# Norms between stages in halves of 512 tokens, with the first three chunks of the next stage fed half by half

## The chip, the cores and the metric

The kernel runs on one core of one Trainium2 chip. The metric is the device time of one execution in microseconds (us), the median of several; lower is better. Engines are named as in the profile: PE is TensorE (matrix products), DVE is VectorE, ACT is ScalarE, POOL is GpSimd, SP is SyncE, which issues most of the DMAs.

## The reference, cut to what matters

The program computes a chain of residual layers over 1024 tokens of width 1024, in float32. Between the large parts it only adds and norms:

```python
for layer in range(2):
    h = rmsnorm(x, mix_pre_g[layer])
    m = even_mixer(h, ...) if layer % 2 == 0 else odd_mixer(h, ...)   # forgetting attention + pooling / gated linear recurrence
    x = x + rmsnorm(m, mix_post_g[layer])
    h = rmsnorm(x, ffn_pre_g[layer])
    x = x + rmsnorm(swiglu(h, w_gate, w_up, w_down), ffn_post_g[layer])
# second block
xn = rmsnorm(x, norm_pre_g);  proj = xn @ w_in
...                                     # mLSTM branch, S5 branch, gates
x = x + rmsnorm(merged @ w_o, norm_post_g)

def rmsnorm(x, g):                      # over the 1024 channels of a token
    return x * rsqrt(mean(x * x, axis=-1) + 1e-6) * g
```

## The kernel before, in words

Activations lie transposed: channels on the 128 partitions, in KT = 8 tiles, the S = 1024 tokens along the free dimension. A product is made from three matrix products of rounded parts (`product`, lines 343 to 345): every operand is split in a high part and a low rest, `H_hi`, `H_lo` for the normed input and `w_hi`, `w_lo` for the weights. Weights come as a stream of chunks of 128x1024: SP loads a chunk into `raw[slot]` (L309), POOL splits it (L331 and L333) as soon as the chunk that used the slot before has been multiplied (semaphore `multiplied`), and PE multiplies it (`columns`): 8 tiles by 2 halves of 512 tokens by 3 products, 48 matmuls into two PSUM banks. There are three slots.

Each engine has its program as a list of stages, run in order: `prelude` (constants for later stages), then boundary b0, `fox` (attention), b1, `ffn(0)`, b2, `lru`, b3, `ffn(1)`, b4, `s5`, `mlstm`, `merge`, b5. Nothing else orders the work: each engine goes through its list, and semaphores tie the lists together.

A boundary takes the last stage's output Y, norms it (`post`), adds it to the residual X (read back from memory; X lies where H_hi and H_lo will be, in b1 in the scratch area), writes X out, norms X (`pre`) and leaves H. b0 has no `post`, b5 no `pre`. In order, for whole tiles 128x1024:

- ACT squares the tiles of Y (L410) as they come, POOL adds the first seven (L476), PE sums over the partitions by 8x8 small matmuls with `pick` (L441); ACT takes the root (L401), DVE the reciprocal (L502), PE spreads it over the partitions into PSUM (L448).
- DVE scales Y tile by tile (L515); DVE adds the even tiles to X (L518), POOL the odd ones (L487).
- ACT squares each new X (L421) and issues its store (L423); PE sums; root, reciprocal, spread again.
- POOL splits the next stage's first three chunks after its last X add.
- DVE scales X (L535), ACT rounds it to H_hi (L430), DVE (even, L529) and POOL (odd, L495) make H_lo. Four tiles of scratch go round.

The first chunk of the next stage waits on PE for each tile of H as it is finished (`ready`); the others follow whole. The next stage's ACT, DVE and, in `s5`, SP programs begin with a wait for `tmp_free`: all of H_lo made and all of X stored. In `s5` that is ahead of the loads of its maps (`s_bn`, `s_cn`) and of all its DVE work (from L1808 on); in `ffn` and `lru` ahead of a memset of Y.

`prelude` runs on DVE before b0: 77 small steps, each waiting for the one before it, then two sines on ACT (L1165, L1166), then 15 more small steps. b0's `tmp_free` condition makes its ACT, DVE and POOL programs wait for the last of them. The first chunk of `fox` holds the gate logits: ACT and DVE turn them into `negc_rows` (L799 to L801, L890 to L894), SP writes those to memory, reads them back, and only then loads chunk 4 and on. The first attention pass on DVE is L946.

Of the kernel before, what the change touches and what calls it, by code (L numbers as in the profile page):

```python
# [194 lines left out]
def block_program(nc, A, out_x):  # L195
# [169 lines left out]
    def boundary(tag, post, pre, src, y_ready, x_free, sq_free, next_chunks=None, x_at=None):  # L365


# [5 lines left out]
            (f"{tag}_spreads", [KT, KT, P], F32), (f"{tag}_roots", [KT, P], F32), (f"{tag}_inverses", [KT, P], F32), keep=14 * S * 4)  # L373
        y_sum = t1
        sq, tmp = (sq0, sq1), (t0, t1, t2, t3)
        stats = int(bool(post)) + int(bool(pre))

        totals = dict(x_loaded=16, x_even=n_post // 2, x_odd=n_post // 2, x_stored=16 * n_post, y_squared=n_post, y_summed=max(0, n_post - 1), squared=n_pre, summed=KT - 1 if pre else 0,
                      all_summed=2 * stats, rooted=stats, inverted=stats, spreads_made=1, y_scaled=n_post,
                      h_full=n_pre, h_hi=n_pre, h_even=n_pre // 2, h_odd=n_pre // 2)  # L380
# [4 lines left out]
        x_new = ("x_even", "x_odd")  # L385

        sums = [ps[0:KT, 4 + 2 * n, 0:P] for n in range(2)]
        first = 0 if post else 1

        def sp(e):  # L390
            for w, v in x_free:
                e.wait_ge(w, v)
            e.dma_start(X[:, :, :], src.rearrange("k p n -> p k n")).then_inc(q["x_loaded"], 16)

        def act(e):
            for w, v in sq_free:
                e.wait_ge(w, v)

            def root(stat):
                e.wait_ge(q["all_summed"], b["all_summed"] + 2 * (stat - first) + 1)  # L400
                e.activation(roots[:, :], sums[stat], ACT.Sqrt, scale=1.0 / D, bias=eps_col[0:KT, :]).then_inc(q["rooted"], 1)  # L401

            e.activation(warm[:, :], eps_col[:, :], ACT.Sqrt)
            if post:
                with e.Fori(0, KT // 2) as i:
                    for t in range(2):
                        k = 2 * i + t
                        e.wait_ge(y_ready[0], y_ready[1] + k + 1)
                        e.wait_ge(q["y_summed"], b["y_summed"] + k + 1)
                        e.activation(sq[t][:, :], tile(Y, k), ACT.Square).then_inc(q["y_squared"], 1)  # L410
                root(0)
            if pre:
                if not post:
                    e.wait_ge(q["x_loaded"], b["x_loaded"] + 16)
                with e.Fori(0, KT // 2) as i:
                    for t in range(2):
                        k = 2 * i + t
                        if post:
                            e.wait_ge(q[x_new[t]], b[x_new[t]] + i + 1 + 2 * t)
                        e.wait_ge(q["summed"], b["summed"] + k + 1)  # L420
                        e.activation(sq[t][:, :], tile(X, k), ACT.Square).then_inc(q["squared"], 1)  # L421
                        if post:
                            e.dma_start(tile(x_dram_t, k), tile(X, k)).then_inc(q["x_stored"], 16)  # L423
                root(1)
                if post:
                    e.wait_ge(q["x_stored"], b["x_stored"] + 16 * KT)
                with e.Fori(0, KT // 4) as i:
                    for t in range(4):
                        e.wait_ge(q["h_full"], b["h_full"] + 4 * i + t + 1)
                        e.activation(tile(H_hi, 4 * i + t), tmp[t][:, :], ACT.Copy).then_inc(q["h_hi"], 1)  # L430
            else:
                with e.Fori(0, KT // 2) as i:
                    for t in range(2):
                        e.wait_ge(q[x_new[t]], b[x_new[t]] + i + 1 + 2 * t)
                        e.dma_start(tile(out_x.rearrange("k p n -> p k n"), 2 * i + t), tile(X, 2 * i + t)).then_inc(q["x_stored"], 16)
                e.wait_ge(q["x_stored"], b["x_stored"] + 16 * KT)

        def pe(e):
            def add(stat, squares, start, stop):
                for m in range(KT):  # L440
                    ins = e.matmul(sums[stat], pick[:, m * KT:(m + 1) * KT], squares[:, m * P:(m + 1) * P], start=start and m == 0, stop=stop and m == KT - 1)  # L441
                return ins

            def spread(stat):
                e.wait_ge(q["spreads_made"], b["spreads_made"] + 1)
                e.wait_ge(q["inverted"], b["inverted"] + stat - first + 1)
                for m in range(KT):
                    ins = e.matmul(ps[:, 2 * stat + m // 4, (m % 4) * P:(m % 4 + 1) * P], spreads[:, m, :], inverses[:, :], start=True, stop=True)  # L448
                ins.then_inc(q["all_summed"], 1)

            if post:
                e.wait_ge(q["y_summed"], b["y_summed"] + KT - 1 + 2)
                e.wait_ge(y_ready[0], y_ready[1] + KT)
                add(0, y_sum, True, False)
                e.wait_ge(q["y_squared"], b["y_squared"] + KT)
                add(0, sq[1], False, True).then_inc(q["all_summed"], 1)
                spread(0)
            if pre:
                for k in range(KT):
                    e.wait_ge(q["squared"], b["squared"] + k + 1)  # L460
                    add(1, sq[k % 2], k == 0, k == KT - 1).then_inc(q["all_summed" if k == KT - 1 else "summed"], 1)
                spread(1)

        def pool(e):
            o = steps_of(e, "pool")
            for w, v in sq_free:
                e.wait_ge(w, v)

            e.tensor_tensor(spreads[:, :, :], ident[0:KT, 0:KT].rearrange("p (m o) -> p m o", o=1).broadcast_to([KT, KT, P]),
                            ones[0:KT, :].rearrange("p (o n) -> p o n", o=1).broadcast_to([KT, KT, P]), ALU.mult).then_inc(q["spreads_made"], 1)  # L470
            if post:
                o(e.memset(y_sum[:, :], 0.0))

                def sum_up(k, squares):
                    e.wait_ge(q["y_squared"], b["y_squared"] + k + 1)
                    e.tensor_tensor(y_sum[:, :], y_sum[:, :], squares[:, :], ALU.add).then_inc(q["y_summed"], 1)  # L476
                    e.wait_ge(q["y_summed"], b["y_summed"] + k + 3)

                with e.Fori(0, KT // 2 - 1) as i:
                    for t in range(2):  # L480
                        sum_up(2 * i + t, sq[t])
                sum_up(KT - 2, sq[0])
                with e.Fori(0, KT // 4) as i:
                    for t in (1, 3):
                        k = 4 * i + t
                        e.wait_ge(q["y_scaled"], b["y_scaled"] + k + 1)
                        e.tensor_tensor(tile(X, k), tile(X, k), tmp[t][:, :], ALU.add).then_inc(q["x_odd"], 1)  # L487
            if next_chunks:
                split_chunks(e, next_chunks, 0, SLOTS)
            if pre:  # L490
                with e.Fori(0, KT // 4) as i:
                    for t in (1, 3):
                        k = 4 * i + t
                        e.wait_ge(q["h_hi"], b["h_hi"] + k + 1)
# [2033 lines left out]
```

## Time and profile before

| | us |
|---|---|
| median of 3 runs | 3793.95 (3792.83 to 3794.66) |
| the profiled execution, its own time | 3794.27 |
| its span, first to last instruction | 3791.4 |
| PE busy | 3459.4 (91%) |
| PE weight loads busy | 2800.8 (74%) |
| DVE busy | 1776.6 (47%) |
| ACT busy | 731.2 (19%) |
| POOL busy | 1540.6 (41%) |
| mean granted clock of TensorE, of its full 2.4 GHz | 0.957 |

The time of an execution is some 3 us longer than the span of its instructions. Busy shares are means over stages of different kinds; matmuls overlap, so a busy PE need not be at its peak. In timelines a row gives start, duration (of all merged pieces, from the first start to the last end or their sum), engine, line, operation, tiles out and in, shape, count, and in brackets the idle time before it and what ended it.

### The profile page before, as it was taken

The numbers are of one execution on the slowest core, as the hardware profiler recorded it, in microseconds if no ns is written. First come the engines' busy times: TensorE is split into PE (matmuls) and PEld (weight loads), VectorE is DVE, ScalarE is ACT, GpSimd is POOL, SyncE is SP. The second block draws the span as 40 slices with busy tenths as digits, with TensorE's granted clock in tenths as the row PEclk, the third lists the DMA queues.
The fourth block names the chain that finished last, engine by engine and source line by source line (L and its number), as shares of the span: only waits on it lengthen the run. The fifth ranks groups of instructions, "written<-read, shape, count | busy, mean of one in ns | idle before, by whom it ended". The sixth has DMA issues, their size and how long they took to land. (4 is left out here: it accounts for less than half of the span.)

```text
span 3791.4 us, 40722 instructions
## 1 busy us (share of the span) xinstructions
PE 3459.4 (91%) x15904; PEld 2800.8 (74%) x15904; DVE 1776.6 (47%) x1746; ACT 731.2 (19%) x923; POOL 1540.6 (41%) x720
## 2 busy tenths in 40 slices
PE   6999898999999979986999999989787999989897
PEld 4777686888888867765888888868666777767685
DVE  4444425332332367675323323259665566565542
ACT  3333312000000033333100000021111223122110
POOL 4111645433443463445434433466642422413255
PEclk9999899999999999997999999989889999999998
DMA  3110022111111221121111111123212210101122
GB/s 102 40 29 26 17 84 73 51 50 50 50 44 50 89 73 39 44 89 56 51 50 50 44 50 44 50 106 89 65 52 78 87 35 28 53 22 53 33 78 105
DMA packets 246568, 215.78 MB, mean 57 GB/s; under 512 B 7988, under 2 KB 213428, under 8 KB 246472
## 3 DMA queue, kind: packets, MB, share of 16 engines
q1 hardware_dynamic: 225888, 165.14, 14.7%
q10 hardware_dynamic: 20584, 49.31, 3.7%
q8 instruction: 66, 1.08, 0.1%
q14 instruction: 30, 0.25, 0.0%
HBM read 180.78 MB, written 29.43 MB: 55 GB/s over the span
## 5 line engine op out<-in xcount | busy, mean ns | idle before, releaser
L331 POOL TENSOR_TENSOR w_hi<-raw,one_col 128x1024 fp32r<-128x1024 f32 x265 | 528.2, 1993 | 1921.2 <-PE ps L345 1866.2
L343 PE MATMUL ps<-H_hi,w_hi 128*128 128x512 f32 x2848 | 1138.7, 400 | 89.1 <-DVE H_lo L529 23.6
L345 PE MATMUL ps<-H_hi,w_lo 128*128 128x512 f32 x2848 | 1119.4, 393 | 0.0
L344 PE MATMUL ps<-H_lo,w_hi 128*128 128x512 f32 x2848 | 1119.0, 393 | 0.0
L343 PEld LDWEIGHTS ps<-H_hi,w_hi 128*128 128x128 f32 x2848 | 541.5, 190 | 218.5 <-issue 49.5
L333 POOL TENSOR_TENSOR w_lo<-raw,w_hi 128x1024 fp32r<-128x1024 f32 x265 | 667.0, 2517 | 20.7
L345 PEld LDWEIGHTS ps<-H_hi,w_lo 128*128 128x128 f32 x2848 | 540.8, 190 | 115.0
L344 PEld LDWEIGHTS ps<-H_lo,w_hi 128*128 128x128 f32 x2848 | 541.9, 190 | 109.0 <-issue 1.9
L1037 DVE TENSOR_TENSOR Y<-Y,ps 128x1024 f32<-128x1024 f32 x176 | 213.0, 1218 | 183.0 <-PE ps L345 183.0
L343 PE MATMUL ps<-ffn_f_hi,w_hi 128*128 128x512 f32 x704 | 273.9, 389 | 0.0
L344 PE MATMUL ps<-ffn_f_lo,w_hi 128*128 128x512 f32 x704 | 273.9, 389 | 0.0
L345 PE MATMUL ps<-ffn_f_hi,w_lo 128*128 128x512 f32 x704 | 273.9, 389 | 0.0
L1027 DVE SCALAR_TENSOR_TENSOR ffn_f<-ffn_a,ps 128x1024 f32<-128x1024 f32 x44 | 53.7, 1221 | 363.4 <-PE ps L345 363.4
L1024 DVE SCALAR_TENSOR_TENSOR ffn_a<-ffn_th,ps 128x1024 f32<-128x1024 f32 x44 | 53.8, 1222 | 349.7 <-ACT ffn_th L1016 349.6
L1016 ACT ACTIVATE ffn_th<-ps 128x1024 f32<-128x1024 f32 x44 | 45.2, 1027 | 754.4 <-PE ps L345 754.4
L1029 DVE TENSOR_TENSOR ffn_f_lo<-ffn_f,ffn_f_hi 128x1024 fp32r<-128x1024 f32 x44 | 138.2, 3142 | 49.6 <-ACT ffn_f_hi L1018 49.6
L345 PEld LDWEIGHTS ps<-ffn_f_hi,w_lo 128*128 128x128 f32 x704 | 132.2, 188 | 27.5
L343 PEld LDWEIGHTS ps<-ffn_f_hi,w_hi 128*128 128x128 f32 x704 | 132.2, 188 | 27.4
L344 PEld LDWEIGHTS ps<-ffn_f_lo,w_hi 128*128 128x128 f32 x704 | 132.2, 188 | 27.4
L1018 ACT ACTIVATE ffn_f_hi<-ffn_f 128x1024 fp32r<-128x1024 f32 x44 | 46.7, 1062 | 482.5 <-DVE ffn_f L1027 482.5
L441 PE MATMUL ps<-b_sq,pick 128*8 128x128 f32 x720 | 89.8, 291 | 49.0 <-ACT b_sq L421 49.0
L441 PEld LDWEIGHTS ps<-b_sq,pick 128*8 128x8 f32 x720 | 68.4, 96 | 69.4 <-issue 27.9
(443 smaller groups left out, 4628.0 us busy)
## 6 DMA issues: line engine op xcount, KB each, us to landing
raw<-in_w_in SPq DMA_DIRECT2D x49, 512.0 KB
raw<-in_ffn_w_gate SPq DMA_DIRECT2D x44, 512.0 KB
raw<-in_ffn_w_up SPq DMA_DIRECT2D x44, 512.0 KB
raw<-in_ffn_w_down SPq DMA_DIRECT2D x44, 512.0 KB
x_dram<-b_X ACTq DMA_DIRECT2D x32, 512.0 KB, 2.6
b_X<-x_dram SPq DMA_DIRECT2D x4, 4096.0 KB, 13.7
raw<-in_ev_w_in SPq DMA_DIRECT2D x17, 512.0 KB
b_X<-in_x_t SPq DMA_DIRECT2D x2, 4096.0 KB, 13.3
```

The costliest lines, as they stand in the source:

```text
L331: pool.tensor_tensor(w_hi[s][:, :n], raw[s][:, :n], one_col[:, :].broadcast_to([P, n]), ALU.mult).then_inc(split_hi, 1)
L333: pool.tensor_tensor(w_lo[s][:, :n], raw[s][:, :n], f32(w_hi[s][:, :n]), ALU.subtract).then_inc(split, 1)
L343: pe.matmul(o, l_hi, r_hi, start=first, stop=False)
L344: pe.matmul(o, l_hi, r_lo, start=False, stop=False)
L345: return pe.matmul(o, l_lo, r_hi, start=False, stop=last)
L441: ins = e.matmul(sums[stat], pick[:, m * KT:(m + 1) * KT], squares[:, m * P:(m + 1) * P], start=start and m == 0, stop=stop and m == KT - 1)
L1016: e.activation(th[t][:, :], pair(2 * t), ACT.Tanh, scale=0.5).then_inc(tanh_done, 1)
L1018: e.activation(f_hi[par_][:, t, :], f[t][:, :], ACT.Copy).then_inc(f_hi_done, 1)
L1024: e.scalar_tensor_tensor(a[t][:, :], th[t][:, :], 1.0, pair(2 * t), ALU.add, ALU.mult).then_inc(gated, 1)
L1027: e.scalar_tensor_tensor(f[t][:, :], a[t][:, :], 0.5, pair(2 * t + 1), ALU.mult, ALU.mult).then_inc(f_full, 1)
L1029: e.tensor_tensor(f_lo[par_][:, t, :], f[t][:, :], f32(f_hi[par_][:, t, :]), ALU.subtract).then_inc(f_ready, 1)
L1037: e.tensor_tensor(Y[:, n, :], Y[:, n, :], pair(n % 4), ALU.add).then_inc(y_added, 1)
```

## The change

Every boundary works in halves of 512 tokens. X is loaded by two DMAs and stored by 16 of half the size. The sums, roots, reciprocals and spreads are made once for each half. On each engine the work of half 0 and half 1 is interleaved in a written-out order; the first three chunks of the next stage are multiplied within the boundary, first for half 0, with the sums of half 1's squares between them, then for half 1. POOL splits chunk 0 before its X adds, chunk 1 behind those of half 0, chunk 2 behind those of half 1. The next stages start at their fourth chunk. `prelude` is no stage any more: its ACT and DVE parts are called within `fox`, behind the gate logits and ahead of q, k and v of the first pair, with scratch at another place; b0 waits for nothing. Some pairs of semaphores in `fox` and `s5` are merged into one, with the counts adapted, and in `s5` the chunk `gt` goes to another bank. The diff, cut to its core:

```diff
@@ boundary @@
+        halves = (slice(0, HALF), slice(HALF, S))
+        squares = [t[:, half] for t in (sq0, sq1) for half in halves]
+        scaled_to = [t[:, half] for t in (t2, t3) for half in halves]
+        full_to = [t[:, half] for t in (t0, t1) for half in halves]
...
         def sp(e):
             for w, v in x_free:
                 e.wait_ge(w, v)
-            e.dma_start(X[:, :, :], src.rearrange("k p n -> p k n")).then_inc(q["x_loaded"], 16)
+            for h in range(2):
+                e.dma_start(X[:, :, halves[h]], src[:, :, halves[h]].rearrange("k p n -> p k n")).then_inc(q[f"x_loaded{h}"], 16)
...
+            def x_square(h, k):
+                i = KT * h + k
+                if post:
+                    x_added(e, h, k)
+                    if i == 0:
+                        wait(e, "y_total", 2)
+                elif k == 0:
+                    wait(e, f"x_loaded{h}", 16)
+                if i >= 4:
+                    wait(e, "summed", i - 3)
+                e.activation(squares[i % 4], X[:, k, halves[h]], ACT.Square).then_inc(q["squared"], 1)
+                if post:
+                    e.dma_start(x_dram_t[:, k, halves[h]], X[:, k, halves[h]]).then_inc(q[f"x_stored{h}"], 16)
...
+                root(0, 0)
+                root(0, 1)
             if pre:
...
+                for k in range(KT):
+                    x_square(0, k)
+                for k in range(2):
+                    x_square(1, k)
+                root(1, 0)
+                for k in range(KT):
+                    h_high(0, k)
+                for k in range(2, KT):
+                    x_square(1, k)
+                root(1, 1)
+                for k in range(KT):
+                    h_high(1, k)
...
+            if post:
+                wait(e, "y_summed", KT - 1)
+                e.wait_ge(y_ready[0], y_ready[1] + KT)
+                wait(e, "y_squared", KT)
+                for h in range(2):
+                    add(0, h, y_sum[:, halves[h]], True, False)
+                    add(0, h, sq1[:, halves[h]], False, True).then_inc(q["y_total"], 1)
+                spread(0, 0)
+                spread(0, 1)
+            if pre:
+                for k in range(KT):
+                    x_add(0, k)
+                for k in range(2):
+                    x_add(1, k)
+                spread(1, 0)
+                part(0, 0, 0, KT)
+                part(0, 1, 0, 4)
+                x_add(1, 2)
+                x_add(1, 3)
+                part(0, 1, 4, KT)
+                x_add(1, 4)
+                x_add(1, 5)
+                part(0, 2, 0, 3)
+                x_add(1, 6)
+                x_add(1, 7)
+                part(0, 2, 3, KT)
+                spread(1, 1)
+                for c in range(3):
+                    part(1, c, 0, KT)
...
+            splits(0)
+            if post:
+                for k in (1, 3, 5, 7):
+                    x_add(0, k)
+            splits(1)
+            if post:
+                x_add(1, 1)
             if pre:
...
+                for k in (1, 3, 5, 7):
+                    h_low(0, k)
+            if post:
+                for k in (3, 5, 7):
+                    x_add(1, k)
+            splits(2)
+            if pre:
+                for k in (1, 3, 5, 7):
+                    h_low(1, k)
...
+            def scale(h, k):
...
+                e.scalar_tensor_tensor(scaled_to[i % 4], Y[:, k, halves[h]], col(post, k), ps[:, post_bank[h], :], ALU.mult, ALU.mult).then_inc(q["y_scaled"], 1)
+                if k % 2 == 0:
+                    wait(e, "y_scaled", i + 1)
+                    e.tensor_tensor(X[:, k, halves[h]], X[:, k, halves[h]], scaled_to[i % 4], ALU.add).then_inc(q["x_even"], 1)
...
+            def h_half(h):
+                inverse(1, h)
+                for k in range(KT):
+                    h_fill(h, k)
+                    if k % 2:
+                        h_low(h, k - 1)
...
+                inverse(0, 0)
+                inverse(0, 1)
+                for k in range(KT):
+                    scale(0, k)
+                for k in range(2 if pre else KT):
+                    scale(1, k)
             if pre:
+                h_half(0)
                 if post:
...
+                    for k in range(2, KT):
+                        scale(1, k)
+                h_half(1)
@@ fox, act @@
             a.step(e.activation(f_abs[:, :], f_abs[:, :], ACT.Ln, bias=one_col[0:8, :]))
+            pl["act"](e)
             e.wait_ge(*done("q0"))
@@ fox, dve @@
             e.tensor_tensor_scan(negc_rows[:, :], ones_rows[:, :], f_min[:, :], 0.0, ALU.mult, ALU.add).then_inc(negc_ready, 1)
+            pl["dve"](e)
             e.wait_ge(qkv_hi, 1)
@@ ffn and lru, pe @@
-            pe_gate_up(e, B, first, 0, 0, ready=h_ready)
+            pe_gate_up(e, B, first, 0, 0, begun=3)
...
-            pe_in(e, 0, first, 0, ready=h_ready)
+            pe_in(e, 0, first, 0, begun=3)
@@ s5, pe @@
-            gemm("u0", ready=h_ready)
-            gemm("u1")
-            gemm("gt", after("u0"))
             gemm("g0", after("u1"))
-            turns(0, 0, "gt")
+            turns(0, 0, "u0")
@@ the list of stages @@
-    b0 = boundary("b0", None, "mix_pre0", A["x_t"], None, [], pl["tmp_free"], "fox")
+    b0 = boundary("b0", None, "mix_pre0", A["x_t"], None, [], [], ("fox", 0))
...
-    steps += [pl, b0, fx, b1, f0, b2, lr, b3, f1, b4, s5_, ml, mg, b5]
+    steps += [b0, fx, b1, f0, b2, lr, b3, f1, b4, s5_, ml, mg, b5]
```

## Rows read from the trace of the kernel before

**Rows 1.** The page's first line.
```profile
span 3791.4 us, 40722 instructions
```
**Rows 2.** Timelines of boundary b1 and the windows view behind it.
```profile
576.10 1.22 DVE L966 COPY Y<-ps 128x1024 f32<-128x1024 f32 x1 [9.65 <-PE ps L345]
...
588.46 3.15 POOL L487 TENSOR_TENSOR b_X<-b_X,b_t 128x1024 f32 x1 [18.35 <-DVE b_t L515]
...
590.70 15.81 PE L441 MATMUL ps<-b_sq,pick 128*8 128x128 f32 x128 [5.28 <-ACT b_sq L421]
...
614.45 0.77 PE L343 MATMUL ps<-H_hi,w_hi 128*128 128x512 f32 x1 [4.31 <-DVE H_lo L529]
...
632.34 1.28 ACT L1016 ACT_TABLE_LOAD   x1 [4.44 <-PE ps L345]
...
632.30:665.00 32.70, 32.70 (x146) 27.09 (x145) 13.78 (x6) 4.40 (x4) 9.63 (x5) 1.00 0.18 49
```
**Rows 3.** The start: the input's DMA (time to landing last), and timeline rows.
```profile
b_X<-in_x_t SPq DMA_DIRECT2D x1, 4096.0 KB, 12.9
...
4.24 0.17 DVE L1110 SCALAR_TENSOR_TENSOR pre_e<-par 128x8 f32<-128x8 f32 x1 [4.24 <-POOL ident_b L2416]
...
21.27 1.28 ACT L1165 ACT_TABLE_LOAD   x1 [21.27 <-DVE pre_small L1140]
...
26.71 2.00 ACT L421 ACTIVATE b_sq<-b_X 128x1024 f32 x2
```
**Rows 4.** Groups by form with 128x512 operands: busy, mean ns.
```profile
L2279 DVE TENSOR_TENSOR ml_st<-ps,ml_E 128x512 f32<-128x512 f32 x24 | 16.6, 692 | 47.6 <-PE ps L2054 44.6 <-DVE ml_em L2260 1.5 <-DVE ml_acc L2265 0.8
...
L2181 ACT ACTIVATE ml_st_hi<-ml_st 128x512 fp32r<-128x512 f32 x24 | 15.1, 629 | 59.1 <-DVE ml_st L2279 59.1
...
L1476 POOL TENSOR_TENSOR s_aB<-s_pw,s_bn 128x512 f32<-128x512 f32 x8 | 9.3, 1162 | 68.5 <-PE ps L1525 62.6 <-DVE s_mag L1836 5.9
```
**Rows 5.** Timelines of DVE and POOL at the same moments, in b2 and in s5.
```profile
1381.94 3.12 DVE L529 TENSOR_TENSOR H_lo<-b_t,H_hi 128x1024 f32 x1
...
1381.63 5.69 POOL L495 TENSOR_TENSOR H_lo<-b_t,H_hi 128x1024 f32 x2
...
2613.76 1.93 DVE L1936 TENSOR_TENSOR s_E<-s_E,s_t 128x64 f32<-128x64 f32 x1
...
2613.72 1.90 POOL L331 TENSOR_TENSOR w_hi<-raw,one_col 128x1024 fp32r<-128x1024 f32 x1
```
**Rows 6.** Timelines of boundary b3: Y's last tile, and ACT after chunk 0's end.
```profile
1746.53 1.22 DVE L1310 TENSOR_TENSOR Y<-Y,ps 128x1024 f32<-128x1024 f32 x1 [1.50 <-PE ps L345]
...
1805.28 1.28 ACT L1016 ACT_TABLE_LOAD   x1 [4.75 <-PE ps L345]
```
**Rows 7.** Timelines of b4 and s5: last Y tile, first DVE work of s5, the first output products.
```profile
2512.05 1.22 DVE L1037 TENSOR_TENSOR Y<-Y,ps 128x1024 f32<-128x1024 f32 x1 [1.50 <-PE ps L345]
...
2566.81 0.14 DVE L1808 MEMSET s_Kp<- 128x96 f32 x1 [2.55 <-POOL H_lo L495]
...
2663.45 2.07 PE L1561 MATMUL ps<-s_Ca,s_s 128*128 128x256 f32 x4 [9.21 <-DVE s_s L1895]
```
**Rows 8.** Timeline of DVE in lru's first head.
```profile
1431.94 0.69 DVE L1278 TENSOR_SCALAR lru_T<-lru_T 128x1024 f32<-128x1024 f32 x1 [8.19 <-ACT lru_T L1234]
```
**Rows 9.** Timelines of b5: first scaling and last add.
```profile
3771.22 2.47 DVE L515 SCALAR_TENSOR_TENSOR b_t<-Y,par,ps 128x1024 f32<-128x1024 f32 x2 [3.57 <-PE ps L448]
...
3785.07 3.15 POOL L487 TENSOR_TENSOR b_X<-b_X,b_t 128x1024 f32 x1 [0.36 <-DVE b_t L515]
```
**Rows 10.** Timelines of fox's start: ACT, DVE, POOL, DVE.
```profile
67.35 1.11 ACT L799 ACTIVATE f_abs<-ps,par 8x1024 f32<-8x1024 f32 x1 [4.40 <-PE ps L345]
...
74.64 2.28 DVE L894 TENSOR_TENSOR_SCAN negc_rows<-ones_rows,f_min 8x1024 f32<-8x1024 f32 x1
...
86.16 1.90 POOL L331 TENSOR_TENSOR w_hi<-raw,one_col 128x1024 fp32r<-128x1024 f32 x1 [14.41 <-DMA raw<-in_ev_w_in]
...
104.32 0.29 DVE L946 CUSTOM_DVE_ANT_0 s<-ps,negc_b 128x128 f32<-128x128 f32 x1
```

More of the change, by code:

```diff
@@ L397, in act, with root @@
                 e.wait_ge(w, v)
-            def root(stat):
-                e.wait_ge(q["all_summed"], b["all_summed"] + 2 * (stat - first) + 1)
-                e.activation(roots[:, :], sums[stat], ACT.Sqrt, scale=1.0 / D, bias=eps_col[0:KT, :]).then_inc(q["rooted"], 1)
+            def root(stat, h):
+                if stat == 0:
+                    wait(e, "y_total", h + 1)
+                else:
+                    wait(e, "summed", KT * h + KT)
+                e.activation(roots[:, h, :], sums(stat, h), ACT.Sqrt, scale=1.0 / D, bias=eps_col[0:KT, :]).then_inc(q["rooted"], 1)
@@ L403, in act, with h_high @@
+            def h_high(h, k):
+                if post and k == 0:
+                    wait(e, f"x_stored{h}", 16 * KT)
+                wait(e, "h_full", KT * h + k + 1)
+                e.activation(H_hi[:, k, halves[h]], full_to[(KT * h + k) % 4], ACT.Copy).then_inc(q["h_hi"], 1)
             e.activation(warm[:, :], eps_col[:, :], ACT.Sqrt)
             if post:
[L405 to L457, printed above, removed]
+                for k in range(KT):
+                    e.wait_ge(y_ready[0], y_ready[1] + k + 1)
+                    if k >= 2:
+                        wait(e, "y_summed", k - 1)
+                    e.activation((sq0, sq1)[k % 2][:, :], Y[:, k, :], ACT.Square).then_inc(q["y_squared"], 1)
@@ new lines, in x_add, with h_low, splits @@
+            def x_add(h, k):
+                i = KT * h + k
+                wait(e, "y_scaled", i + 1)
+                e.tensor_tensor(X[:, k, halves[h]], X[:, k, halves[h]], scaled_to[i % 4], ALU.add).then_inc(q["x_odd"], 1)
+            def h_low(h, k):
+                i = KT * h + k
+                wait(e, "h_hi", i + 1)
+                e.tensor_tensor(H_lo[:, k, halves[h]], full_to[i % 4], f32(H_hi[:, k, halves[h]]), ALU.subtract).then_inc(q["h_odd"], 1)
+            def splits(c):
+                if seam:
+                    split_chunks(e, seam[0], seam[1] + c, seam[1] + c + 1)
@@ new lines, in h_fill @@
+            def h_fill(h, k):
+                i = KT * h + k
+                if k == 0:
+                    wait(e, "spread", number(1, h))
+                    if h == 0 and post:
+                        wait(e, "y_total", 2)
+                if post:
+                    x_added(e, h, k)
+                if i >= 4:
+                    wait(e, ("h_even", "h_odd")[k % 2], 4 * ((i - 4) // KT) + (i - 4) % KT // 2 + 1)
+                e.scalar_tensor_tensor(full_to[i % 4], X[:, k, halves[h]], col(pre, k), ps[:, pre_bank[h], :], ALU.mult, ALU.mult).then_inc(q["h_full"], 1)
@@ L655, in pe @@
         def pe(e):
-            def whole(name, b, ready=None):
-                j = chunk[name]
-                e.wait_ge(split, stream.number(N, j))
-                columns(e, stream.slot(N, j), b, H_hi, H_lo, ready=ready).then_inc(multiplied, 1)
             def half_chunk(name, h):
@@ L717, in pools @@
                     yield from mixing(i)
-            whole("f", 0, h_ready)
-            whole("q0", 1)
-            whole("k0", 2)
-            whole("v0", 3)
+            e.wait_ge(split, stream.number(N, chunk["v0"]))
+            columns(e, stream.slot(N, chunk["v0"]), 3, H_hi, H_lo).then_inc(multiplied, 1)
             e.wait_ge(vt_ready, 1)
```

287 lines of the change are left out of this document (144 added, 143 removed).

## The prediction

> **What bounds the kernel now.** I read the page first [rows 1]: TensorE is busy in 9 tenths of nearly every slice, and the slices that are lower are the start, the ends of stages and the latency-bound stages. So I read the boundaries b0 to b5 as timelines. In b1 the last output tile of the attention leaves TensorE at E = 576.10 and the first product of the feed-forward stage starts at 614.45, E+38.4; DVE, GpSimd and the square sums (128 records from 590.70 to 606.5, paced by TensorE) fill the time in between. Chunk 0, fed tile by tile, is over at 632.3 = E+56.2, and then TensorE runs without a gap, 10.9 us a chunk (144 matmuls in 32.7 us) [rows 2]. So chunks 0 to 2 are over at E+56.2+21.8 = E+78.0. That is the number the change must beat, four times (b1 to b4). At b0 the first square waits until 26.71 for the constants, though the input needs 12.9 us to land after an issue at 2.1; 77 vector steps run from 4.24 to 21.2, sines follow, then 15 steps [rows 3].
>
> **Prices of half tiles.** A 128x512 two-input DVE operation takes 0.69 us (0.61 from start to start), an ACT pass 0.63, a GpSimd one 1.16 [rows 4]. Their whole-tile forms cost 1.22, 1.06 and about 2.3, so a half is a little over half and splitting alone costs only some 0.1 us an operation. What costs more is order. While GpSimd runs an operation on SBUF, a DVE operation with both inputs in SBUF does not proceed: DVE's H_lo starts at 1381.94, just after GpSimd's at 1381.63, and lasts 3.12 instead of 1.22, the rest of GpSimd's 2.3 and then its own (GpSimd's second, behind it in turn, makes 5.69 of two times 2.3); the 128x64 step at 2613.76 lasts 1.93 instead of 0.2, to the end of GpSimd's 1.90 from 2613.72 [rows 5]. The same the other way: GpSimd's X add at 588.46 lasts 3.15, its own 2.3 after a DVE add of the same kind that runs until 589.4 [rows 2]. The scaling passes, which read one side from PSUM, go on beside it.
>
> **A boundary, half by half (b1, from E).** (1) The sums of Y wait for the last square but are halved, as is the spread: the first scale can start at about E+7.6 (an estimate: some 2 us before it does now, and 2 us more are lost if that isn't so). (2) Scaling: per two tiles DVE does scale, add, scale, and GpSimd one add. The add of the even tile now comes right behind its own scale, when GpSimd has just begun the odd tile's add: it waits, and a pair takes 0.61+0.2+1.16+0.69 = 2.7 us, not 0.61x2+0.69 = 1.9. Half 0 is added at 7.6+1.3+3x2.7+0.7+1.4 = E+19.0. (3) GpSimd then splits chunk 1 (1.9+2.4 and one held DVE add: to E+23.9) before x_add(1,1), E+25.1, on which square, root, reciprocal and spread of half 0 hang by the program order of ACT and TensorE: 4.2 us (0.6 for the square, the rest an estimate from one root, one reciprocal and a half spread), E+29.3. Scale, hi and lo of the first tile 2.4: first product at E+31.7, 6.7 us earlier than before. (4) Half 0 of H comes at 1.1 us a tile, 8.7 us (TensorE alone would need 5.5): E+40.4. Only now does DVE scale the other six halves, three pairs, and GpSimd is done adding at E+47.5; its split of chunk 2 ends at E+51.9. TensorE has half of chunk 1 (5.5) and four square sums (0.88 each), is through at E+49.4 and waits 2.5. Then 8 tiles of chunk 2, two sums and a spread: 5.5+1.8+1.2, E+60.3. (5) Bubble for the first tile of half 1, 2.8; half 1 of chunk 0 again at H's pace, 8.6; half 1 of chunks 1 and 2, 10.9: E+82.6. Against E+78.0 that is 4.6 us lost at b1. Cross-check: the early start gives 6.7 and H's pace 0.5 (17.8-10.9 = 6.9 of stall in chunk 0 before, 8.7+8.6-10.9 = 6.4 after); six sums and a spread inside the product take 6.5, the wait for chunk 2's split 2.5, the second bubble 2.8: 4.6 lost.
>
> **b3** was slower before: chunk 0 over 58.7 after its E [rows 6], 2.5 more than in b1. If the changed one takes what b1's does, 4.6-2.5 = 2.1 are lost, and 4.6 if what delays it comes back.
>
> **b4: who waits for all of H.** The next stage's DVE work and the DMAs of its maps wait until the last H_lo: 2566.81, E+54.8 [rows 7]. With the halves that is E+70.8. From there a chain of DVE work without a gap, other than some 4 us for the maps, ends in s_s, for which TensorE has already waited 9.21 us at 2663.45 [rows 7]. So 16.0 us more ahead of that chain are 16.0 us on the kernel; that TensorE finished chunks 0 to 2 at a slightly other time doesn't matter there. No row speaks for an absorption; the bound from the other side is that a few held operations vanish (2 us).
>
> **b2** has the same shift of 16, and its DVE chain of convolution and gate leads to an activation for which TensorE waits later too; but DVE sits idle 8.19 before chunk 3's square is there [rows 8]. 16.0-8.2 = 7.8, less 0.8 because chunk 3 itself is less late than H: 7.0 lost.
>
> **b5** has only the first part. Its scaling starts 3.6 earlier (half of the spreads operation, sums and reciprocal ahead of the second half's), but eight pairs take 1.3+7x2.7+0.7+1.4 = 22.2, where the four took 3788.2-3771.2 = 17.0 [rows 9]; the last store is half as large (0.4): 0.8 lost.
>
> **b0 and the constants.** Half of the input should be there at about 9.9 (estimate: half of its stream). Sums, root, spread: H starts at 22.6, the first product at 25.9. GpSimd splits two chunks first, and the weights land behind the input (16.5 to 25.1, an estimate): it just fits. By the steps above chunk 0 is over at 63.1, chunks 1 and 2 at 74.0, chunk 3 at 84.9, where before chunk 0 was over at 67.35 and chunk 3 at 99.9. So far 15 us gained. But the gate chain (9.6 us, 67.35 to 76.92) ends at 72.7 and only then do the constants run on DVE, with q, k and v of the first pair queued behind them on DVE and, behind the sines, on ACT. In the first 9.2 us, 44 of the 77 steps are done. Then the next weights land, as 9.2 us after the chain before [rows 10], and GpSimd runs three splits, six instructions, 13.3 us, to 95.2. Each lets about one small DVE step through; some 8 pass, 25 remain: 101.1. Table load and sines 2.0, ACT's q, k, v 3.0, transposes and v_hi 2.2, v_lo and start 1.7: first softmax pass at about 110.0 against 104.32 [rows 10]: 5.7 lost. If nothing held these steps, they'd end at 88.8 and the pass would start at 97.7: 6.6 gained. Those are the bounds; I take the first since 2613.76 is exactly such a step.
>
> The row shows this only for two-input steps; 18 of the 33 are one-input. The Trainium skill (GPSIMD Engine Reference, Specifications) says that GpSimd shares its SBUF interfaces with VectorE, in contention with instructions "in a 2-port perf mode or with two SBUF inputs". By it the one-input steps are held too, and by the row alone perhaps 22 rather than 25 remain, 0.6 us less.
>
> **Sum:** 5.7+4.6+7.0+2.1+16.0+0.8 = 36.2 us on the profiled execution (span 3791.4, its time 3794.27; the median of the runs is 3793.95, 0.3 below it): 3830.
>
> **Rivals.** (A) The holds don't bite: pairs take 1.9 us and the constants pass between the splits. Then chunk 2 is over at about E+79, H complete at E+66.9: b0 +6.6, b1 -0.8, b2 -3.3, b3 +1.4, b4 -12.3, b5 +3.6, in all 5 lost: 3799. For it: in the kernel before most H_lo of the two engines pass each other untouched, and small shifts in order decide. (B) Faster: TensorE isn't starved once it has begun. H's half 1 would have to follow half 0 so closely that neither split nor second bubble shows: chunk 2 is then over at 31.7+32.7+6.5+4 = E+74.9, 3.1 gained at b1 and 5.6 at b3; H complete at E+63 leaves b2 even (8.2 of slack) and costs 8.2 at b4; b0 11 gained, b5 3.6: 15 gained, 3779. It turns faster by 0.2% where, with the constants free, H is complete before about E+65. Against it: the program order puts scaling of the six halves behind all of half 0. (C) The s5 chain absorbs most of its shift, since TensorE's and GpSimd's work there gets out of its way: 3816. (D) More goes wrong: the split of chunk 3 lands late, since chunk 1's slot is now free only 5.5 us after chunk 0's, 2 us at each of four places, and DVE's steps slow further: 3845.
>
> **How the numbers follow.** The sum as worked out 0.50, C 0.08, D 0.08, A 0.20 (it ends near the bound, a third of it on the slow side), B 0.14. 0.2% is 7.6 us, about what a measurement of this kernel can tell. Slower 0.70, same 0.16, faster 0.14. The range, 3792 to 3846, reaches from A's fast side to D; the sum's own is 3816 to 3844 (2 us a boundary, 4 at b0 and b4).
>
> **What would show it.** First product of b1 near E+31.7, a bubble of 2 to 3 us behind the second spread, chunks 0, 1, 2 ending 5.5 apart with the last near E+82.6; DVE adds of about 1.5 us beside GpSimd's; the sines near 101 and the first softmax pass near 110; in s5 a wait for s_s above 12 us. It is wrong if small DVE steps pass GpSimd's splits, if H is complete before E+65, or if s_s comes no later after b4.

## The result and the profile after

| | before | changed |
|---|---|---|
| median | 3794.3 us (3792.83 to 3797.76, 4 runs) | 3825.57 us (3819.97 to 3828.08, 4 runs) |
| ratio | | 1.0079, 95% interval 1.0062 to 1.0097 |
| span of the profiled execution | 3791.4 | 3818.2 |

The change makes the kernel slower by 31 us, 0.8%, and the interval lies clear of 1; 3830 was forecast, with a range of 3792 to 3846. The profiled execution of the changed kernel is the fastest of its four (3819.97), so it was profiled and timed once more in the experiments (`n_again`: 3825.42 us, ratio 1.0076, interval 1.006 to 1.0093, span 3823.7). Rows below are of the first execution. E is again the start of the last tile of Y, and "the hold" is what the prediction describes: an operation of DVE or GpSimd that does not proceed while the other engine's operation runs.

The page's first line, then the timelines of DVE: the first softmax pass, and the last tile of Y ahead of b1 to b5 (start, duration, ...). The distances between them, compared with the same points in the kernel before [rows 2, 6, 7, 10], say where the time went.

```profile
span 3818.2 us, 40162 instructions
...
109.05 0.29 DVE L1034 CUSTOM_DVE_ANT_0 s<-ps,negc_b 128x128 f32<-128x128 f32 x1
...
582.24 1.22 DVE L1054 COPY Y<-ps 128x1024 f32<-128x1024 f32 x1 [9.66 <-PE ps L345]
...
1348.87 1.22 DVE L1125 TENSOR_TENSOR Y<-Y,ps 128x1024 f32<-128x1024 f32 x1 [1.50 <-PE ps L345]
...
1759.00 1.22 DVE L1399 TENSOR_TENSOR Y<-Y,ps 128x1024 f32<-128x1024 f32 x1 [1.50 <-PE ps L345]
...
2525.55 1.22 DVE L1125 TENSOR_TENSOR Y<-Y,ps 128x1024 f32<-128x1024 f32 x1 [1.50 <-PE ps L345]
...
3785.51 1.23 DVE L2477 COPY Y<-ps 128x1024 f32 x1 [9.65 <-PE ps L345]
```

Of the kernel before, two more such points, which were not shown, and two rows that the text below needs (timelines of DVE and POOL):

```profile
1339.39 1.22 DVE L1037 TENSOR_TENSOR Y<-Y,ps 128x1024 f32<-128x1024 f32 x1 [1.50 <-PE ps L345]
...
1397.40 6.88 DVE L1347 MEMSET Y<- 128x8192 f32 x1 [4.25 <-issue]
...
3756.08 1.23 DVE L2392 COPY Y<-ps 128x1024 f32 x1 [9.65 <-PE ps L345]
...
3757.74 2.34 POOL L476 TENSOR_TENSOR b_t<-b_t,b_sq 128x1024 f32<-128x1024 f32 x1 [0.23 <-POOL b_t L476]
```

| us lost (- gained) | forecast | first execution | `n_again` |
|---|---|---|---|
| b0, to the first softmax pass | 5.7 | 4.7 | 4.6 |
| attention, pass to last Y tile | 0 | 1.4 | 3.1 |
| b1 and ffn(0) | 4.6 | 3.3 | 3.3 |
| b2 and lru | 7.0 | 3.0 | 6.8 |
| b3 and ffn(1) | 2.1 | 1.0 | 0.9 |
| b4, s5 to merge | 16.0 | 15.9 | 16.2 |
| b5 | 0.8 | -2.6 | -2.6 |
| sum of spans | 36.2 | 26.8 | 32.3 |

Each measured entry is a difference of two distances: for b1, (1348.87-582.24)-(1339.39-576.10) = 766.63-763.29 = 3.3.

**b0.** Timelines of DVE, POOL and ACT behind the gate logits. The one-input step that starts 0.07 after GpSimd's split takes 1.85 instead of 0.18, and six two-input steps beside the next splits take 6.92, where six such steps took 1.27 at 75.09. ACT loads the table of the sines at 69.89, while it waits, and not behind the steps:

```profile
75.09 1.27 DVE L1192 SCALAR_TENSOR_TENSOR pre_r<-pre_r,pre_e 128x24 f32<-128x24 f32 x6
...
83.18 0.17 DVE L1186 TENSOR_SCALAR pre_n<-pre_u 128x16 f32<-128x16 f32 x1
83.39 1.85 DVE L1187 TENSOR_SCALAR pre_n<-pre_n 128x16 f32<-128x16 f32 x1
...
89.57 6.92 DVE L1192 SCALAR_TENSOR_TENSOR pre_r<-pre_r,pre_u 128x16 f32<-128x16 f32 x6
...
83.32 1.90 POOL L331 TENSOR_TENSOR w_hi<-raw,one_col 128x1024 fp32r<-128x1024 f32 x1 [15.00 <-DMA raw<-in_ev_w_in]
...
69.89 1.28 ACT L1253 ACT_TABLE_LOAD   x1
...
101.36 0.34 ACT L1253 ACTIVATE rot_im<-pre_theta 128x160 f32<-128x160 f32 x1 [30.19 <-DVE pre_small L1229]
```

**b1.** Timelines of DVE, POOL, PE and ACT. A pair of half tiles starts every 2.55 us (592.36 to 594.91); DVE's add takes 1.20 and GpSimd's 1.27. TensorE starts its product at 613.58, waits 1.65 for the split of chunk 2 and 2.29 for the first H_lo of half 1, and is through chunk 0 at 652.67:

```profile
592.36 1.20 DVE L593 TENSOR_TENSOR b_X<-b_X,b_t 128x512 f32<-128x512 f32 x1
593.49 1.39 DVE L590 SCALAR_TENSOR_TENSOR b_t<-Y,par,ps 128x512 f32<-128x512 f32 x2
594.91 1.20 DVE L593 TENSOR_TENSOR b_X<-b_X,b_t 128x512 f32<-128x512 f32 x1
...
591.75 1.26 POOL L540 TENSOR_TENSOR b_X<-b_X,b_t 128x512 f32<-128x512 f32 x1 [11.28 <-DVE b_t L590]
594.30 1.27 POOL L540 TENSOR_TENSOR b_X<-b_X,b_t 128x512 f32<-128x512 f32 x1 [1.29 <-DVE b_t L590]
...
613.58 0.77 PE L343 MATMUL ps<-H_hi,w_hi 128*128 128x512 f32 x1 [2.38 <-DVE H_lo L610]
...
632.91 0.50 PE L343 MATMUL ps<-H_hi,w_hi 128*128 128x512 f32 x1 [1.65 <-POOL w_lo L333]
...
644.09 0.80 PE L343 MATMUL ps<-H_hi,w_hi 128*128 128x512 f32 x1 [2.29 <-DVE H_lo L610]
...
652.67 1.28 ACT L1104 ACT_TABLE_LOAD   x1 [2.56 <-PE ps L345]
```

**b4 and s5.** Timelines of DVE and PE. The first DVE work of s5 stands 71.0 after the last Y tile (54.8 before), and TensorE's long waits are now four:

```profile
2596.58 0.14 DVE L1893 MEMSET s_Kp<- 128x96 f32 x1 [1.43 <-POOL H_lo L545]
...
2610.47 0.47 PE L343 MATMUL ps<-H_hi,w_hi 128*128 128x512 f32 x1 [2.09 <-ACT s_ub L1742]
...
2626.89 1.94 PE L1613 MATMUL ps<-ident,s_aB 128*128 128x128 f32 x8 [5.28 <-POOL s_aB L1572]
...
2632.92 0.79 PE L343 MATMUL ps<-H_hi,w_hi 128*128 128x512 f32 x1 [4.08 <-POOL w_lo L333]
...
2693.50 2.07 PE L1649 MATMUL ps<-s_Ca,s_s 128*128 128x256 f32 x4 [6.61 <-DVE s_s L1980]
```

### The profile page after: what moved, and what is told of

Read it like the earlier page. It is cut to its first block and busy times, and to the rows that moved or that the text cites. A ratio compares the mean times of both kernels' runs of the same rounds, so it can differ in the third digit from the quotient of the medians.

```text
span 3818.2 us, 40162 instructions
## 1 busy us (share of the span) xinstructions
PE 3478.4 (91%) x15904; PEld 2800.7 (73%) x15904; DVE 1826.4 (48%) x1876; ACT 747.1 (20%) x1013; POOL 1521.6 (40%) x760
## 3 DMA queue, kind: packets, MB, share of 16 engines
q1 hardware_dynamic: 232128, 165.14, 14.8%
## 5 line engine op out<-in xcount | busy, mean ns | idle before, releaser
L343 PE MATMUL ps<-H_hi,w_hi 128*128 128x512 f32 x2848 | 1145.5, 402 | 88.9 <-DVE H_lo L610 24.2
L1104 ACT ACTIVATE ffn_th<-ps 128x1024 f32<-128x1024 f32 x44 | 45.2, 1027 | 738.1 <-PE ps L345 738.1
L1117 DVE TENSOR_TENSOR ffn_f_lo<-ffn_f,ffn_f_hi 128x1024 fp32r<-128x1024 f32 x44 | 137.1, 3116 | 49.6 <-ACT ffn_f_hi L1106 49.6
L472 PE MATMUL ps<-b_sq,pick 128*8 128x128 f32 x720 | 101.3, 303 | 34.0 <-ACT b_sq L429 33.9
L472 PEld LDWEIGHTS ps<-b_sq,pick 128*8 128x8 f32 x720 | 68.7, 99 | 64.3 <-ACT b_sq L429 28.8
```

The lines of the kernel that those rows point to most:

```text
L343: pe.matmul(o, l_hi, r_hi, start=first, stop=False)
L472: ins = e.matmul(sums(stat, h), pick[:, m * KT:(m + 1) * KT], source[:, m * P:(m + 1) * P], start=start and m == 0, stop=stop and m == 3)
L1104: e.activation(th[t][:, :], pair(2 * t), ACT.Tanh, scale=0.5).then_inc(tanh_done, 1)
L1117: e.tensor_tensor(f_lo[par_][:, t, :], f[t][:, :], f32(f_hi[par_][:, t, :]), ALU.subtract).then_inc(f_ready, 1)
```

## The experiments

All are edits of the changed kernel unless said otherwise; "faster" is against its 3825.57. The ratios are to the kernel before, whose median was 3794.93 to 3795.04 beside them.

**1. `a_splits_wait`: does GpSimd hold the small steps?** GpSimd splits chunks 4 to 6 only after all 92 steps.

```diff
-            split_chunks(e, N, SLOTS, chunk["u2"] + 1)
+            split_chunks(e, N, SLOTS, SLOTS + 1)
+            e.wait_ge(sem("dve_order"), pl["made"])
+            split_chunks(e, N, SLOTS + 1, chunk["u2"] + 1)
...
-        return dict(dve=dve, act=act)
+        return dict(dve=dve, act=act, made=angles_made + 15)
```

> The changed kernel, with one wait more: GpSimd splits the weight chunks 4, 5 and 6 of the attention stage only after DVE has made all 92 steps of the constants. Theory of the hold (while GpSimd runs a two-input operation on SBUF, DVE's small steps don't proceed): with no split beside them the 77 steps take the 17.0 us that they took at the start of the kernel before, 73.4 to 90.4, sines to 91.4, the last 15 steps to 94.6, first softmax pass at 98.8 instead of 109.05, and the kernel 10 us faster than the changed one. Rival (their place in the order of DVE costs, not the hold): the pass stays at 109 within 2 us and the kernel where it is, or slower, since the splits come 11 us later.

3812.97 us, ratio 1.0049 (1.0033 to 1.0066): 12.6 faster, although all that is changed is that work is made to wait. The sines start at 90.09 and the first pass at 97.79:

```profile
90.09 0.34 ACT L1255 ACTIVATE rot_im<-pre_theta 128x160 f32<-128x160 f32 x1 [19.18 <-DVE pre_small L1231]
...
97.79 0.29 DVE L1036 CUSTOM_DVE_ANT_0 s<-ps,negc_b 128x128 f32<-128x128 f32 x1
```

The hold is shown, and it cost 11.3 us at this place. The pass was expected at 98.8 and the gain at 10.

**2. `b_const_b0`: the first 60 steps where DVE is idle.** The function is cut behind the second exponential.

```diff
+        def dve_rest(e):
+            o = dve_steps(e)
+            lr, li = vec("lam_re", 16), vec("lam_im", 16)
             for k in range(1, POWERS):
...
-            pl["dve"](e)
+            pl["dve_rest"](e)
...
-    steps += [b0, fx, b1, f0, b2, lr, b3, f1, b4, s5_, ml, mg, b5]
+    steps += [dict(dve=pl["dve"]), b0, fx, b1, f0, b2, lr, b3, f1, b4, s5_, ml, mg, b5]
```

> The changed kernel, but the first 60 of the 92 steps of the constants run on DVE ahead of b0's first reciprocal, where DVE is idle until 21.07; the other 32 and the sines stay behind the gate logits. By the hold and the queue together: 60 steps of 0.22 from 4.2 end at 17.4, just as GpSimd's first split starts, so b0 is not later; behind the gate chain (73.4) 17 steps end at 77.8, the sines at 78.5, the rest at 81.7, ahead of GpSimd's splits at 83.3. Then q, k and v wait for TensorE alone (chunk 3 over at 85.6), first softmax pass at 90.0 instead of 109.05: 19 us faster than the changed kernel. If b0's root comes late because steps are held by the first splits: 17 us. Rival (something else than the constants holds the first pass, such as the rows of the gate that go through memory): 5 us or less.

3804.18 us, ratio 1.0026 (1.0015 to 1.0036): 21.4 faster. The reciprocal of b0 isn't late (20.21, 21.07 in the changed kernel), and the pass starts at 90.06 as expected. Against `n_again`, 18.9 of the profile's 24.2 us lie there; 3.4 more lie in b4 to merge (1256.8 instead of 1260.2), which was not expected and whose cause stays open.

```profile
17.35 0.18 DVE L1194 SCALAR_TENSOR_TENSOR mag<-pre_r,pre_bits 128x16 f32<-128x16 f32 x1
20.21 0.94 DVE L581 RECIPROCAL b_inverses<-b_roots 8x128 f32<-8x128 f32 x1 [2.69 <-ACT b_roots L417]
...
90.06 0.28 DVE L1034 CUSTOM_DVE_ANT_0 s<-ps,negc_b 128x128 f32<-128x128 f32 x1
```

**3. `c_pairs`: DVE adds behind two scalings.**

```diff
-                if k % 2 == 0:
-                    wait(e, "y_scaled", i + 1)
-                    e.tensor_tensor(X[:, k, halves[h]], X[:, k, halves[h]], scaled_to[i % 4], ALU.add).then_inc(q["x_even"], 1)
+                if k % 2:
+                    wait(e, "y_scaled", i)
+                    e.tensor_tensor(X[:, k - 1, halves[h]], X[:, k - 1, halves[h]], scaled_to[(i - 1) % 4], ALU.add).then_inc(q["x_even"], 1)
```

> The changed kernel, but DVE scales two half tiles and then adds the even one, in place of scale, add, scale. By the hold: DVE's add then goes ahead of GpSimd's and takes 0.69 instead of a mean of 1.14, a pair takes 1.9 instead of 2.55 us. In b1 first product at E+28.7 instead of E+31.3, chunk 2's split 4.5 earlier, chunk 2 over at E+76.8 instead of E+81.3; b1, b3 and b4 gain 4.5 each, b2 4, b5 5: 22 us faster than the changed kernel. Rival (1.2 is simply what the add costs beside GpSimd, in whatever order): pairs stay at 2.5, 0 within 3 us.

3800.18 us, ratio 1.0011 (1.0001 to 1.0021): 25.4 faster, by the order of two instructions. Against `n_again`, b1 and ffn(0) take 762.1 instead of 766.6, b3 and ffn(1) 761.7 instead of 766.5, b4 to merge 1254.5 instead of 1260.2, b5 4.7 less, and b2 and lru 408.2 instead of 413.9 (the first execution's low 410.1 is no measure here, see experiment 9). The groups by form, of the changed kernel and then of this one (count | busy, mean ns):

```profile
L540 POOL TENSOR_TENSOR b_X<-b_X,b_t 128x512 f32<-128x512 f32 x40 | 50.8, 1270 | 71.4 <-DVE b_t L590 71.4
...
L593 DVE TENSOR_TENSOR b_X<-b_X,b_t 128x512 f32<-128x512 f32 x40 | 45.4, 1136 | 1.4
```

```profile
L540 POOL TENSOR_TENSOR b_X<-b_X,b_t 128x512 f32<-128x512 f32 x40 | 64.9, 1622 | 35.1 <-DVE b_t L590 34.7
L593 DVE TENSOR_TENSOR b_X<-b_X,b_t 128x512 f32<-128x512 f32 x40 | 27.1, 677 | 0.0
```

DVE's add now goes first and costs its own 0.68; it is GpSimd's, 1.27 before, that is held to 1.62 in the mean.

**4. `d_straight_b4`: no interleaving in b4.** All 16 half tiles are scaled and added, then H is made in a row; TensorE does chunk 0 in both halves first. GpSimd's splits move too: chunk 1 behind all its adds, chunk 2 behind its last H_lo. TensorE's order in b4:

```diff
+                    for k in range(2, KT):
+                        x_add(1, k)
+                    spread(1, 0)
+                    part(0, 0, 0, 4)
+                    spread(1, 1)
+                    part(0, 0, 4, KT)
+                    part(1, 0, 0, KT)
+                    for c in (1, 2):
+                        part(0, c, 0, KT)
+                        part(1, c, 0, KT)
```

> The changed kernel, but in b4 alone the halves are not interleaved: all 16 half tiles are scaled and added, then H is made for half 0 and half 1 in a row, TensorE finishes chunk 0 before chunk 1. Pairs of 2.55 end at E+29.1, H complete at E+49.5 instead of E+69.7, chunks 0 to 2 over at E+72.3 instead of E+81.3. By the theory that the next stage's DVE chain from all of H sets the end of b4: 19 us faster than the changed kernel, 4 us better at this place than the kernel before. Rival (TensorE's own chunks set it): 9 us. Rival (the chain is absorbed): under 5 us.

3806.73 us, ratio 1.0033 (1.0022 to 1.0045): 18.8 faster. With the last Y tile at 2529.23, H is complete 51.9 later (71.0 in the changed kernel), and the way from that tile to the one ahead of b5 is 1239.6 instead of 1260.0. That is 20.4 less, the whole 19.2 by which H is earlier, and not the 9 that the expectation gave to TensorE's chunks.

```profile
2581.08 0.14 DVE L1923 MEMSET s_Kp<- 128x96 f32 x1 [1.45 <-POOL H_lo L563]
```

**5. `e_const_back`: the constants ahead of b0 again.**

```diff
-            pl["act"](e)
...
-            pl["dve"](e)
...
-    b0 = boundary("b0", None, "mix_pre0", A["x_t"], None, [], [], ("fox", 0))
+    b0 = boundary("b0", None, "mix_pre0", A["x_t"], None, [], pl["tmp_free"], ("fox", 0))
...
-    steps += [b0, fx, b1, f0, b2, lr, b3, f1, b4, s5_, ml, mg, b5]
+    steps += [pl, b0, fx, b1, f0, b2, lr, b3, f1, b4, s5_, ml, mg, b5]
```

> The changed kernel with the constants back where they were: a stage of their own ahead of b0, which waits for them. Theory: the first square waits until 26.7 instead of 10.1, so b0's half-by-half work moves by 16.6 less what GpSimd's finished splits no longer hold: chunk 3 over near 101 to 102 instead of 85.6, first softmax pass at 105.5 to 106.6 instead of 109.05, 3 us faster than the changed kernel: moving the constants as the change does it was worth nothing. Rival (the constants ahead of b0 cost their full 16 us): 12 us or more slower than the changed kernel.

3819.77 us, ratio 1.0064 (1.0047 to 1.0081), which the interval does not tell from the changed kernel; its first pass starts at 105.95, 3.1 earlier. Moving the constants, as it was done, bought nothing.

**6. `g_straight_all`: experiment 4 in b1 to b4.**

> The changed kernel with the halves in a row in b1 to b4, and nothing else. Theory: b1 and b3 gain 9 each (chunks 0 to 2 over at E+72.3 instead of E+81.3), b4 20.4 as measured alone, b2 9 to 12 (its DVE chain starts 20 earlier, but TensorE's chunk 3 only 9): 47 to 50 us faster than the changed kernel, near 3777. Rival (the start of H, 2.2 later in a row than interleaved, counts in b1 and b3): b1 and b3 lose 2 each, 28 us.

3775.98 us, ratio 0.9948 (0.9932 to 0.9965): 49.6 faster, where 47 to 50 was expected. Its parts fall differently: against `n_again` b1 gains 6.3, b2 14.6, b3 8.2 and b4 19.4, where 9, 9 to 12, 9 and 20.4 were expected.

**7. `h_interleaved` and `f_best`: the two repairs with and without the interleaving.** The first is experiments 2 and 3 together, the second 2, 3 and 6.

> The change's interleaved halves with the two repairs that leave the interleaving alone (60 steps of the constants in b0, scaling in pairs). Both were worth 21.4 and 25.4 us alone; if they add up: 46 us faster than the changed kernel, near 3779, 15 faster than the kernel before. What is then left to the kernel with the halves in a row is the cost of the interleaving: 50 us by the theory. Rival (the two share a wait): 35 us or less faster than the changed kernel.

> All together: the first 60 steps of the constants in DVE's idle time in b0, scaling in pairs, and the halves in a row in b1 to b4 (scale and add all 16 half tiles, then H for half 0 and half 1, chunk 0 before chunk 1). Theory: against the kernel before b0 gains 12.5 (as measured alone), in b1 adds over at E+24.4, H complete at E+44.5, chunk 0 over at E+45.6 instead of E+56.2: b1 10.6, b3 13, b2 12, b4 10, b5 7.3 gained, in all 65 us faster than the kernel before, near 3729. Rival (the stages behind b2 and b4 are bound by TensorE there, and the gain in the chain of DVE work is not passed on): 45 us.

`h_interleaved`: 3780.34 us, ratio 0.9953 (0.9936 to 0.997), 45.2 faster where 46 was expected. `f_best`: 3737.44 us, ratio 0.9849 (0.9833 to 0.9865), 57.6 faster than the kernel before and the best of both; 65 was expected. The missing 7 lie mostly in b1, which gained 6.4 instead of 10.6 and where DVE idles 4.47 between the adds and H. The difference of the two, 42.9 us, is what the interleaving costs, with the places of the splits that go with it; the four runs of `h_interleaved` spread over 12.7 us (3771.14 to 3783.88), so the last digits mean nothing.

```profile
593.53 1.41 DVE L632 SCALAR_TENSOR_TENSOR b_t<-b_X,par,ps 128x512 f32<-128x512 f32 x2 [4.47 <-PE ps L486]
...
614.21 6.88 DVE L1187 MEMSET Y<- 128x8192 f32 x1 [3.12 <-issue]
```

**8. `k_early`: `f_best` with its statistics pulled forward.**

> The kernel of f_best with its statistics pulled forward: DVE's reciprocal of half 1 of Y behind the fourth scaling instead of ahead of all, TensorE's spread of half 0 ahead of the sums of half 1, in the second norm the spread of half 0 ahead of the last two square sums, and the root of half 1 behind the second H_hi. Theory (what is left between the last add and H is this latency: 4.5 us of idle DVE at 593.53 in b1, and a first scaling 9.3 after E instead of 7.4): 1.4 us at five boundaries and 3 at four, 19 us faster than f_best, near 3718. Rival (TensorE's own pace through H, 1.02 us a half tile on DVE, sets it): under 8 us.

3744.61 us (3738.98 to 3750.44), ratio 0.987 (0.9852 to 0.9888): a miss, 7 slower than `f_best`, where 19 faster was expected. Its runs fall in two pairs, near 3739 and 3750; the profile is of one at 3739.07, so it speaks for the 3.8 that this one is behind `f_best`'s (3735.3), and what the other pair loses stays open. In b1 it did what it should (that memset starts 47.9 after the last Y tile instead of 50.4). In b4 the second spread is now late for DVE (2.30), and H's first H_lo meets GpSimd's split and takes 2.28: H is complete 50.0 after Y there, 46.2 in `f_best`, and b4 to merge takes 5.2 longer.

```profile
2488.17 1.41 DVE L623 SCALAR_TENSOR_TENSOR b_t<-Y,par,ps 128x512 f32<-128x512 f32 x2 [2.30 <-PE ps L487]
...
2499.59 2.28 DVE L643 TENSOR_TENSOR H_lo<-b_t,H_hi 128x512 fp32r<-128x512 f32 x1
```

**9. `n_again`: the changed kernel, unchanged.**

> The changed kernel again, unchanged. Its profiled execution was 5.6 us below its own median, and the four variants that leave b2 and the lru stage as they are took 412.2 to 414.2 us from the last Y tile before b2 to the one before b3, where that execution took 410.1. Theory (that stage falls differently from one execution to the next): it takes 412 to 414 here, with a time near 3825. Rival (the 5.6 us lie in what the profile doesn't see): 410 again, with a time near 3825 all the same.

3825.42 us; from the Y tile before b2 to that before b3 it took 413.9. So the low 410.1 was that one execution's. In b2 its first scaling started 9.0 after the last Y tile, in the first execution 7.4, which is 1.6 of the 3.8.

## Why the prediction was right, step by step

The total held, 3825.57 against 3830, and so did the mechanism of the large terms. Against `n_again` the sum is 3.9 too high: b0 to b4 together 3.6 too much, b5 another 3.4, and the attention stage 3.1 too little, so misses on both sides partly cancel, which is luck.

- **The hold**, which set 2.7 us a pair and the 110.0 of the first pass: right. 2.55 and 109.05 were measured. Within a pair the parts differ: DVE's add starts 0.6 after GpSimd's (592.36 and 591.75), not 0.2, so it takes 1.20 and not 1.5. At b0 the steps end at 101.3 as forecast (101.1), but "table load and sines 2.0" took 0.5, to 101.83, since the load was long over. Less 0.2 and 0.3 that other steps took more, that is the 1.0 by which the lost 4.7 lies below 5.7. Experiment 1 takes the hold away at b0 and finds 97.79. The forecast's other bound was 97.7, but so close a match is luck: the steps end 1.3 later than it had them (90.1 and 88.8), and the load gives 1.5 back. Experiment 3 takes the hold from DVE's adds. The Trainium skill (GPSIMD Engine Reference, Specifications) says that the contention takes in instructions "in a 2-port perf mode". The trace agrees in that a one-input step is held, 1.85 at 83.39; in which mode it runs, no run shows.
- **b1**: right in each step. Half 0 is added at E+18.4 (19.0 forecast), the first product at E+31.3 (31.7), TensorE waits 1.65 and 2.29 (2.5 and 2.8), H is complete at E+69.2 (70.8), chunk 2 over at E+81.3, from 652.67 and 10.9 (82.6). Lost 3.3 instead of 4.6, b3 1.0 instead of 2.1: in b1 the two waits were put 1.4 too long together, which is the whole difference.
- **b4**: right, 15.9 and 16.2 against 16.0, and experiment 4 shows the cause. Its sign in the profile was forecast wrongly: the wait for s_s was to grow above 12 and fell to 6.61. TensorE is stopped earlier instead. GpSimd's products for `s_aB` wait for the same DVE chain, and the splits of weights stand behind them in GpSimd's order, so TensorE waits 5.28 and then 4.08 there, and 2.09 for `s_ub`. The four are 18.1, against one long wait of 9.21 before; in `n_again` they are 2.43, 2.85, 4.96 and 4.58, 14.8 in all, and the stage lost 16.2 all the same.
- **b2**: right by luck in part. The shift was taken from b4, with H complete at E+54.8 before. In b2 it was complete at E+56.2 before (the end of the row below), and at E+68.7 in the first execution, E+70.8 in `n_again`. So the shift is 12.5 and 14.6, not 16.0. The memset behind H says the same: it stands 1.8 behind the last H_lo in each (1397.40 before). Less the slack of 8.2 that leaves 4.3 and 6.4, and 3.0 and 6.8 were lost. Timelines of GpSimd, before and then changed:

```profile
1393.19 2.38 POOL L495 TENSOR_TENSOR H_lo<-b_t,H_hi 128x1024 f32 x1 [1.34 <-ACT H_hi L430]
```

```profile
1416.30 1.29 POOL L545 TENSOR_TENSOR H_lo<-b_t,H_hi 128x512 fp32r<-128x512 f32 x1 [0.76 <-ACT H_hi L437]
```

- **b5**: the failed term, -2.6 for 0.8. Its own parts add up to 1.2 and not to 0.8 (22.2-17.0-3.6-0.4). The scaling starts 9.0 after Y instead of 15.1, so 6.2 earlier and not 3.6. One part of that was overlooked: GpSimd's sums of Y's squares, written out instead of looped and with a smaller `spreads`, end at E+2.1 instead of E+4.0, and TensorE's sums start at E+2.5 instead of E+4.1. That is 1.6 of the 2.6; the other 1.0 stays open. Eight pairs take 21.2 instead of 22.2, so 4.2 more than before and not 5.2, and 0.7 less lies behind the last add: -6.2+4.2-0.7 is -2.6 within rounding. Timelines of TensorE before, then of GpSimd, TensorE and DVE in the changed kernel:

```profile
3760.13 3.58 PE L441 MATMUL ps<-b_t,pick 128*8 128x128 f32 x16 [4.20 <-POOL b_t L476]
```

```profile
3770.06 17.57 POOL L557 TENSOR_TENSOR b_t<-b_t,b_sq 128x1024 f32<-128x1024 f32 x7
...
3787.97 1.87 PE L472 MATMUL ps<-b_t,pick 128*8 128x128 f32 x8 [2.62 <-ACT b_sq L445]
...
3794.48 0.64 DVE L590 SCALAR_TENSOR_TENSOR b_t<-Y,par,ps 128x512 f32<-128x512 f32 x1
```

- **The attention stage** was put at nothing and lost 1.4 and 3.1; every variant shows 1.3 to 4.0 (473.1 to 475.8 from pass to last Y tile, 471.8 before), and the unchanged repeat alone differs by 1.7. Its cause stays open; nothing here separates the merged semaphores from where the first splits fall.
- **The rivals.** (A), no hold, is ruled out by experiments 1 and 3. Its 3799 is about what `c_pairs` gives, but by chance, since `c_pairs` leaves the constants held. Two of its terms are also off by 0.2 and 0.3 (66.9-54.8 is 12.1 at b4, 2.5-0.8 is 1.7 at b3). (B), TensorE not starved, fails on TensorE's own waits in b1. (C), absorption in s5, fails on experiment 4. (D), chunk 3 split late, does not occur: in b1 to b3 TensorE has no wait for a split at chunk 3.

## What to carry to other kernels

Work that is cut finer to start TensorE earlier gains only if what closes the stage is not later. Here the first product of b1 came 7 us sooner and all of H 12 to 16 us later in b1 to b4, and the chain that waits for all of H in b4 paid in full; the same halves taken in a row won 43 us over the interleaved ones. Where VectorE and GpSimd work on SBUF at the same time, look who goes first: the order of one add was worth 25 us, the place of 60 small steps 21. Small steps that depend on one another belong where GpSimd is silent.

## What the runs showed of the hardware beyond that

The same sums over Y run at either level of TensorE's clock from one execution to the next. In b2, after the same pause of 2.5 us behind the last product, the first eight small matmuls took 1.87 in `n_again` and 1.03 in the first execution. The granted clock over the ten us from the last Y tile was 0.83 and 0.93, that is with more or less of the time at 1.2 instead of 2.4 GHz. First `n_again`, then the first execution, each a timeline row and a window (columns: window, its length, busy us of PE, PEld, DVE, ACT, POOL, clock, DMA share, GB/s):

```profile
1352.88 1.87 PE L472 MATMUL ps<-b_t,pick 128*8 128x128 f32 x8 [2.50 <-ACT b_sq L445]
...
1350.42:1360.42 10.00, 7.11 (x47) 5.35 (x48) 4.03 (x5) 1.77 (x3) 6.22 (x3) 0.83 0.19 54
```

```profile
1351.32 1.03 PE L472 MATMUL ps<-b_t,pick 128*8 128x128 f32 x8 [2.49 <-ACT b_sq L445]
...
1348.87:1358.87 10.00, 6.38 (x51) 5.11 (x52) 5.59 (x7) 2.40 (x4) 6.71 (x4) 0.93 0.22 67
```

The first scaling starts 9.0 after the last Y tile in `n_again` and 7.4 in the first execution. One execution's profile can lie 5 us from the median of such a kernel, so terms of 1 to 3 us are read from more than one.
